# High halves of the weights by a converting DMA instead of a GpSimd pass, in a hybrid decoder trunk on one Trainium2 core

## The chip, the core and the metric

The kernel runs on one core of a Trainium2 chip. The metric is the device time of one execution in microseconds (us), the median of several runs. The engines are named as in the profile: PE is TensorE (PEld its weight loads), DVE is VectorE, ACT is ScalarE, POOL is GpSimd, SP is SyncE, and SPq and ACTq are the instructions with which SP and ACT issue DMAs. They run side by side and wait for each other on semaphores.

## The reference

Two layers of a decoder trunk over 512 tokens of width 2048, in float32. Each layer has one wide input projection, four parallel token mixers (linear attention, windowed attention, differential attention, gated delta rule), a gate on each, and one output projection added to the input:

```python
def hybrid_layer(x, norm_g, w_in, w_out, ...):
    h = rms_norm(x, norm_g)
    p = jnp.einsum('btd,dp->btp', h, w_in)               # 2048 x 7192 weights
    ...
    ya = gla_mixer(...) * jax.nn.silu(az)
    yb = swa_mixer(...) * jax.nn.silu(bz)
    yc = diff_mixer(...) * jax.nn.silu(cz)
    yd = gdn_mixer(...) * jax.nn.silu(dz)
    y = jnp.concatenate([ya, yb, yc, yd], axis=-1)
    return x + jnp.einsum('btm,md->btd', y, w_out)       # 2048 x 2048 weights

def reference(x, ...):
    for l in range(2):
        x = hybrid_layer(x, norm_g[l], w_in[l], w_out[l], ...)
    return x
```

The output is the (1, 512, 2048) array x. The time lies in the two projections and in the chains of small operations inside the mixers.

## The kernel before

**Precision by halves.** A projection in float32 is made of three matmuls on a reduced type that the program calls float32r. A weight w is split into a high half, w rounded to float32r, and a low half, w minus the high half. The activations are split in the same way (actT_hi, actT_lo). The product is hi*hi + hi*lo + lo*hi, so each tile of weights costs three matmuls for each block of 128 rows.

**The weight stream.** All weights of a layer lie in DRAM as a stream of k-tiles of 128x512 float32, two to a pair, 144 pairs a layer, 288 in all. SP loads pair i into the ring w_raw (RAW slots of a pair each) with one DMA of 512 KB (L313) and signals raw_in. POOL then makes both halves of each k-tile: L376 adds zero to w_raw and writes w_hi, which rounds it; L380 subtracts w_hi from w_raw and writes w_lo, and signals w_ready. The rings w_hi and w_lo have RING = 4 k-tiles each. POOL may write a k-tile's slot when PE has finished the k-tile four before it; PE signals this with kt_done, whose value starts at 4. After each pair POOL gives the slot of w_raw back through raw_used, on which SP waits (L311).

**The order on PE.** The function project runs one chunk of the projection: 16 k-tiles for the input (12 or 4 for the output), and for each k-tile 12 matmuls of 128x512 (four blocks of rows, three terms) on L421 into the accumulators acc[0] to acc[3]. Projections 0 to 3 of a layer run bare: the chunks dq, dk, dv of the gated delta rule, and dz. From projection 4 on, a generator (mixer) puts the matmuls of a mixer between those of the projection at fixed places: four projections with gdn, four with gla, two with swa, four output projections with dif, then four short ones of 4 k-tiles.

**What stands beside it.** A project may begin when acc[0] to acc[3] have been read out (acc_free). For dq, dk and dv DVE reads them out itself (turned_out, L1232) and then runs the convolution and its activation (conv): for each of four blocks of 128x512, a scaling (L1252), three shifted multiply-adds (L1256), an exponential on ACT (L916), an addition of one (L1260), a reciprocal (L1263) and a product (L1265). DVE's order is fixed by the text of the program: conv("dk") stands before turned_out("dv"). In gdn the first step of a block on PE (L451) waits for a product that DVE makes (AG, L1303); in swa PE (L660) waits for a copy by DVE (L1461) that stands behind a gate (L1197, L1199, L1201) and the normalisation of the next block (L1424, L1425, L1429).

**The start.** SP issues, in this order, two small constants, then x in four pieces of 1 MB (x_in, L309) with pairs 0 to 3 of the weights between them (L313). PE transposes x (turn_x, L729) before the first k-tiles, and again ahead of later ones.

Of the kernel before, what the change touches and what calls it, by code (L numbers as in the profile page):

```python
# [7 lines left out]
F32 = mybir.dt.float32  # L8
# [31 lines left out]
RAW, RING = 4, 4  # L40
# [73 lines left out]
def hybrid_trunk(nc, x, wstream, wsmall, pcol, prow, wlr, cf, masks, out):  # L114
    ctx = ExitStack()
    with ctx:
# [11 lines left out]
        w_hi = sb("w_hi", [P, RING, GW], F32R)  # L128
# [105 lines left out]
        raw_used, hi_done, w_ready = sem("raw_used"), sem("hi_done"), sem("w_ready")  # L234
# [68 lines left out]
        def _(sp):  # L303
# [7 lines left out]
            def weights(i):  # L311
                sp.wait_ge(raw_used, i + 1)
                sp.dma_start(w_raw[:, i % RAW].rearrange("p a n -> p (a n)"),  # L313
                             wstream[i:i + 1].rearrange("a p n -> p (a n)")).then_inc(raw_in[i % RAW], 16)
# [8 lines left out]
            weights(3)  # L323
# [10 lines left out]
        def _(pool):  # L334

            pool.sem_inc(raw_used, RAW)
# [25 lines left out]

            for l in range(DEPTH):
                for i in range(PAIRS):
                    s = i % RAW
# [5 lines left out]
                    pool.wait_ge(raw_in[s], (l * (PAIRS // RAW) + i // RAW) * 16 + 16)  # L371
                    for k in range(2):
                        n, r = 2 * i + k, (2 * i + k) % RING

                        pool.wait_ge(kt_done, l * LAYER_KTS + (n + 1))
                        pool.tensor_tensor(w_hi[:, r], w_raw[:, s, k], zeros[:, :].broadcast_to([P, GW]), ALU.add) \  # L376
                            .then_inc(hi_done, 1)

                        pool.wait_ge(hi_done, l * LAYER_KTS + (n + 1))
                        pool.tensor_tensor(w_lo[:, r], w_raw[:, s, k], w_hi[:, r].bitcast(F32),  # L380
                                           ALU.subtract).then_inc(w_ready, 1)

                    pool.wait_ge(w_ready, l * LAYER_KTS + (2 * i + 2))
                    pool.sem_inc(raw_used, 1)
# [3 lines left out]
        def _(pe):  # L388
# [7 lines left out]
            def project(l, q, kt0, kts, act_kt, turned=False, ahead=None, mixer=None, stages=1, skip=0,  # L396
# [5 lines left out]
                for k in range(kts):  # L402
                    if ahead:
                        ahead(k)
                    r = (kt0 + k) % RING

                    pe.wait_ge(w_ready, l * LAYER_KTS + (kt0 + k + 1))
                    for b in range(4):
# [5 lines left out]
                        if turned:  # L414
                            terms = [(w_hi[:, r, c], actT_hi[:, a]), (w_hi[:, r, c], actT_lo[:, a]),
                                     (w_lo[:, r, c], actT_hi[:, a])]
                        else:
                            terms = [(actT_hi[:, a, c], w_hi[:, r]), (actT_hi[:, a, c], w_lo[:, r]),
                                     (actT_lo[:, a, c], w_hi[:, r])]
# [1192 lines left out]
```

## Time and profile before

| | |
|---|---|
| median of 3 runs | 2127.36 us (2125.7 to 2127.44) |
| the profiled execution, its own time | 2127.9 us |
| its span in the profile | 2126.1 us |
| PE busy | 2038.3 us, 96% of the span |
| POOL busy | 1396.3 us, 66% |
| DVE busy | 1026.4 us, 48% |
| ACT busy | 537.6 us, 25% |
| DMA | 175.92 MB, 83 GB/s on average |
| granted PE clock, mean | 0.989 of full speed |

The span is what the profiler saw from the first to the last instruction; 1.8 us of the execution's time lie around it. Matmuls overlap each other, so the duration of one on the profile is longer than the step from one to the next. Idle time is counted before the instruction that ended it, with the instruction that released it. The granted clock is the share of full speed that TensorE's throttle allowed: 1.00 is 2.4 GHz and 0.50 is 1.2 GHz.

### The profile page before, as it was taken

What the parts mean: (1) busy time and instruction counts of PE and PEld (TensorE: products, weight loads), DVE (VectorE), ACT (ScalarE), POOL (GpSimd) and SP (SyncE); (2) the same over time, 40 slices, a digit from 0 to 9 for tenths busy, and PEclk for the clock granted to TensorE, in tenths of its full rate; (3) what the DMA queues carried; (4) which work ended last, traced back from release to release, by engine and by line L of the source; (5) the groups of instructions that cost most, each with busy time, mean ns of one, the idle gap of its engine ahead of it and who ended that gap; (6) DMA issues with size and microseconds to landing.
All of it is one profiled execution on the core that took longest, in us unless ns stands there. A gap on an engine that the chain in (4) does not pass through costs nothing.

```text
span 2126.1 us, 25561 instructions
## 1 busy us (share of the span) xinstructions
PE 2038.3 (96%) x10300; PEld 1660.6 (78%) x10300; DVE 1026.4 (48%) x1407; ACT 537.6 (25%) x1014; POOL 1396.3 (66%) x1164
## 2 busy tenths in 40 slices
PE   7998999999999989999999999999999999999999
PEld 6877878878888878767888778778778787776777
DVE  1699453453222455565427984435432225545563
ACT  4010221222222443332320112221222225423220
POOL 6797654555777756557787975545557777555676
PEclk9999999999999999999999999999999999999999
DMA  5232211211222211422442322111122222132223
GB/s 216 74 96 80 70 60 50 60 60 60 80 81 88 80 60 63 146 69 80 129 132 72 99 79 63 57 60 59 51 62 87 80 80 84 55 127 81 74 85 119
DMA packets 50709, 175.92 MB, mean 83 GB/s; under 512 B 5566, under 2 KB 6304, under 8 KB 49568
## 3 DMA queue, kind: packets, MB, share of 16 engines
q1 hardware_dynamic: 44288, 155.75, 23.3%
q10 hardware_dynamic: 6304, 18.55, 2.3%
q8 instruction: 81, 1.33, 0.3%
q14 instruction: 36, 0.29, 0.0%
HBM read 165.89 MB, written 8.39 MB: 82 GB/s over the span
## 4 chain that ended last, share of the span: by engine, by line
PE 72%; DVE 20%; ACT 5%; issue 2%; DMA 1%; SPq 0%; ACTq 0%
PE acc L421 55%; DVE slots L1256 3%; DVE slots L1199 3%; DVE general L1263 3%; PE mix L488 2%; PE mix L499 1%; PE mix L682 1%; PE mix L660 1%; PE mix L528 1%; PE mix L491 1%; DVE slots L1252 1%; ACT slots L849 1%; DVE general L1319 1%; DVE slots L1429 1%; PE mix L774 1%
## 5 line engine op out<-in xcount | busy, mean ns | idle before, releaser
L376 POOL TENSOR_TENSOR w_hi<-w_raw,zeros 128x512 fp32r<-128x512 f32 x576 | 626.2, 1087 | 671.5 <-PE acc L421 648.2
L421 PE MATMUL acc<-w_hi,actT_hi 128*128 128x512 f32 x1920 | 789.0, 411 | 14.0 <-DVE slots L1232 12.1
L380 POOL TENSOR_TENSOR w_lo<-w_raw,w_hi 128x512 fp32r<-128x512 f32 x576 | 767.6, 1333 | 45.1
L421 PE MATMUL acc<-w_hi,actT_lo 128*128 128x512 f32 x1920 | 755.3, 393 | 0.0
L421 PE MATMUL acc<-w_lo,actT_hi 128*128 128x512 f32 x1920 | 753.5, 392 | 0.0
L421 PEld LDWEIGHTS acc<-w_hi,actT_hi 128*128 128x128 f32 x1920 | 364.9, 190 | 106.6 <-issue 38.7
L421 PEld LDWEIGHTS acc<-w_hi,actT_lo 128*128 128x128 f32 x1920 | 363.2, 189 | 80.3
L421 PEld LDWEIGHTS acc<-w_lo,actT_hi 128*128 128x128 f32 x1920 | 365.3, 190 | 65.5
L421 PE MATMUL acc<-actT_hi,w_hi 128*128 128x512 f32 x384 | 153.2, 399 | 2.9 <-DVE slots L1232 2.9
L421 PE MATMUL acc<-actT_hi,w_lo 128*128 128x512 f32 x384 | 150.4, 392 | 0.0
L421 PE MATMUL acc<-actT_lo,w_hi 128*128 128x512 f32 x384 | 150.4, 392 | 0.0
L849 ACT ACTIVATE slots<-acc,xr 128x512 f32<-128x512 f32 x88 | 60.2, 689 | 267.8 <-PE acc L421 267.7
L1199 DVE RECIPROCAL slots<-slots 128x512 f32<-128x512 f32 x32 | 107.3, 3353 | 1.1
L1256 DVE SCALAR_TENSOR_TENSOR slots<-slots,pcol_all 128x511 f32<-128x511 f32 (+2 forms) x72 | 99.1, 1376 | 2.6
L421 PEld LDWEIGHTS acc<-actT_hi,w_hi 128*128 128x128 f32 x384 | 72.7, 189 | 18.8 <-issue 2.2
L421 PEld LDWEIGHTS acc<-actT_hi,w_lo 128*128 128x128 f32 x384 | 72.6, 189 | 15.5
L421 PEld LDWEIGHTS acc<-actT_lo,w_hi 128*128 128x128 f32 x384 | 72.7, 189 | 15.0 <-issue 0.5
L1263 DVE RECIPROCAL general<-general 128x512 f32<-128x512 f32 x24 | 80.5, 3353 | 0.8
L916 ACT ACTIVATE general<-slots 128x512 f32<-128x512 f32 x24 | 15.2, 632 | 252.8 <-DVE slots L1256 252.8
L974 ACT ACTIVATE slots<-mix 128x512 f32<-128x512 f32 x40 | 24.0, 599 | 216.1 <-PE mix L488 216.1
L1480 DVE TENSOR_TENSOR slots<-acc,slots 128x512 f32<-128x512 f32 x64 | 42.7, 688 | 67.4 <-PE acc L421 67.4
L1376 DVE SCALAR_TENSOR_TENSOR slots<-mix,slots 128x256 f32<-128x256 f32 x8 | 3.4, 424 | 139.7 <-ACT slots L999 139.7
(250 smaller groups left out, 2095.5 us busy)
## 6 DMA issues: line engine op xcount, KB each, us to landing
w_raw<-in_wstream SPq DMA_DIRECT2D x288, 512.0 KB, 3.5
out_x<-slots ACTq DMA_DIRECT2D x7, 1024.0 KB, 4.4
slots<-in_x SPq DMA_DIRECT2D x4, 1024.0 KB, 14.5
slots<-in_x ACTq DMA_DIRECT2D x1, 4096.0 KB, 14.2
slots<-out_x ACTq DMA_DIRECT2D x1, 4096.0 KB, 15.0
out_x<-slots ACTq DMA_DIRECT2D x4, 256.0 KB, 2.3
cf_sb<-in_cf ACTq DMA_DIRECT2D x1, 964.0 KB, 11.4
slots<-in_masks ACTq DMA_DIRECT2D x1, 384.0 KB, 12.2
```

The lines of the kernel that those rows point to most:

```text
L376: pool.tensor_tensor(w_hi[:, r], w_raw[:, s, k], zeros[:, :].broadcast_to([P, GW]), ALU.add) \
L380: pool.tensor_tensor(w_lo[:, r], w_raw[:, s, k], w_hi[:, r].bitcast(F32), ALU.subtract).then_inc(w_ready, 1)
L421: last = nc.tensor.matmul(acc[b][:, :], lhsT, rhs, start=(k == 0 and i == 0), stop=(k == kts - 1 and i == 2))
L488: last = nc.tensor.matmul(mh[3][:, h], U["MT"][:, h], U["X"][:, h], start=True, stop=True)
L491: last = nc.tensor.transpose(mh[1][:, h], U["X"][:, h], ident)
L499: last = nc.tensor.matmul(mh[0][:, h], U["XT"][:, h], U["Y"][:, h], start=True, stop=True)
L849: nc.scalar.activation(slot(SLOT[c])[:, b], acc[b][:, :], ACT.Copy, scale=xr[:, l, b:b + 1]) \
L974: nc.scalar.activation(U["Y"], mh[3], ACT.Copy).then_inc(*s(f"y{lv}"))
L1199: dve.reciprocal(tmp, tmp).then_inc(St.sem, St.one(f"{t}.g2"))
L1256: dve.scalar_tensor_tensor(dst[:, d:], src[:, 0:SEQ - d], tap[i], dst[:, d:], ALU.mult, ALU.add).then_inc(*ci(f"t{i}"))
L1263: dve.reciprocal(general[:, b % 2], general[:, b % 2]).then_inc(*ci("rec"))
L1480: dve.tensor_tensor(xs, acc[b][:, :], xs, ALU.add).then_inc(acc_free, 1)
```

## The change

The pass that makes the high half (L376) is gone from POOL. Instead POOL issues, for each pair, a second DMA from the same place in DRAM, from float32 into the float32r tile w_hi, so that the DMA converts. Only POOL's queue issues such a DMA here. w_hi becomes a ring of HI = 3 pairs with a semaphore for each slot (hi_in); w_raw shrinks from 4 pairs to 3, w_lo keeps its 4 k-tiles. The DMA for pair g + 1 is issued after the low half of the first k-tile of pair g; from g + 1 = 3 on it first waits until PE has finished the pair that held its slot. SP no longer waits for raw_used: it waits for w_ready, the low halves of the pair three before. PE only reads the high half from its new place.

```diff
-RAW, RING = 4, 4
+RAW, HI, RING = 3, 3, 4
...
-        w_hi = sb("w_hi", [P, RING, GW], F32R)
+        w_hi = sb("w_hi", [P, HI, 2, GW], F32R)
...
-        raw_used, hi_done, w_ready = sem("raw_used"), sem("hi_done"), sem("w_ready")
+        hi_in = [sem(f"hi_in{i}") for i in range(HI)]
+        w_ready = sem("w_ready")
...
             def weights(i):
-                sp.wait_ge(raw_used, i + 1)
+                if i >= RAW:
+                    sp.wait_ge(w_ready, 2 * (i - RAW) + 2)
                 sp.dma_start(w_raw[:, i % RAW].rearrange("p a n -> p (a n)"),
                              wstream[i:i + 1].rearrange("a p n -> p (a n)")).then_inc(raw_in[i % RAW], 16)
...
             x_in(3)
-            weights(3)
...
+            def high_halves(g):
+
+                if g >= HI:
+                    pool.wait_ge(kt_done, RING + 2 * (g - HI) + 2)
+                pool.dma_start(w_hi[:, g % HI].rearrange("p a n -> p (a n)"),
+                               wstream[g:g + 1].rearrange("a p n -> p (a n)")).then_inc(hi_in[g % HI], 16)
+
+            high_halves(0)
             for l in range(DEPTH):
                 for i in range(PAIRS):
-                    s = i % RAW
+                    g = l * PAIRS + i
...
-                    pool.wait_ge(raw_in[s], (l * (PAIRS // RAW) + i // RAW) * 16 + 16)
+                    pool.wait_ge(raw_in[g % RAW], g // RAW * 16 + 16)
+                    pool.wait_ge(hi_in[g % HI], g // HI * 16 + 16)
                     for k in range(2):
-                        n, r = 2 * i + k, (2 * i + k) % RING
-
-                        pool.wait_ge(kt_done, l * LAYER_KTS + (n + 1))
-                        pool.tensor_tensor(w_hi[:, r], w_raw[:, s, k], zeros[:, :].broadcast_to([P, GW]), ALU.add) \
-                            .then_inc(hi_done, 1)
-
-                        pool.wait_ge(hi_done, l * LAYER_KTS + (n + 1))
-                        pool.tensor_tensor(w_lo[:, r], w_raw[:, s, k], w_hi[:, r].bitcast(F32),
+                        n = 2 * g + k
+
+                        pool.wait_ge(kt_done, n + 1)
+                        pool.tensor_tensor(w_lo[:, n % RING], w_raw[:, g % RAW, k], w_hi[:, g % HI, k].bitcast(F32),
                                            ALU.subtract).then_inc(w_ready, 1)
-
-                    pool.wait_ge(w_ready, l * LAYER_KTS + (2 * i + 2))
-                    pool.sem_inc(raw_used, 1)
+                        if k == 0 and g + 1 < DEPTH * PAIRS:
+                            high_halves(g + 1)
...
-                    r = (kt0 + k) % RING
+                    n = l * LAYER_KTS + kt0 + k
+                    hi, lo = w_hi[:, n // 2 % HI, n % 2], w_lo[:, n % RING]
```

**POOL in the middle of a projection.** Before, one pair is four passes, and the next pair begins with the fifth row:

```order
L376 TENSOR_TENSOR w_hi<-w_raw,zeros 128x512 [waits w_ready,kt_done,raw_in3]
L380 TENSOR_TENSOR w_lo<-w_raw,w_hi 128x512 [waits hi_done]
L376 TENSOR_TENSOR w_hi<-w_raw,zeros 128x512 [waits kt_done]
L380 TENSOR_TENSOR w_lo<-w_raw,w_hi 128x512 [waits hi_done]
L376 TENSOR_TENSOR w_hi<-w_raw,zeros 128x512 [waits w_ready,kt_done,raw_in0]
```

After the change, one pair is two passes and the issue of a DMA (L367), which fetches the high halves of the next pair; the fourth row is the next pair's first:

```order
L385 TENSOR_TENSOR w_lo<-w_raw,w_hi 128x512 [waits kt_done,hi_in0,raw_in0]
L367 DMA w_hi<-in_wstream 128x1024 [waits kt_done]
L385 TENSOR_TENSOR w_lo<-w_raw,w_hi 128x512 [waits kt_done]
L385 TENSOR_TENSOR w_lo<-w_raw,w_hi 128x512 [waits kt_done,hi_in1,raw_in1]
L367 DMA w_hi<-in_wstream 128x1024 [waits kt_done]
```

Two passes that read SBUF have gone from each pair, and the first pass of a pair now also waits for a DMA (hi_in) that POOL issued one pass before.

**POOL at the start of the program.** Before, POOL waits for the first pair of weights with nothing issued:

```order
L338 MEMSET zeros 128x1
L339 MEMSET ws_hl 128x80
L376 ISA
L376 TENSOR_TENSOR w_hi<-w_raw,zeros 128x512 [waits kt_done,raw_in0,zeros_done]
L380 TENSOR_TENSOR w_lo<-w_raw,w_hi 128x512 [waits hi_done]
```

After it, the DMA of pair 0 goes out first:

```order
L338 MEMSET zeros 128x1
L339 MEMSET ws_hl 128x80
L367 DMA w_hi<-in_wstream 128x1024 [waits zeros_done]
L385 ISA
L385 TENSOR_TENSOR w_lo<-w_raw,w_hi 128x512 [waits kt_done,hi_in0,raw_in0]
L367 DMA w_hi<-in_wstream 128x1024
L385 TENSOR_TENSOR w_lo<-w_raw,w_hi 128x512 [waits kt_done]
```

The half megabyte of pair 0 (high) now moves beside the first pieces of x, and that of pair 1 follows after POOL's first pass, without a wait. On SP the fourth load of weights, which stood right behind the last piece of x, now waits for w_ready.

## Rows read from the trace of the kernel before

**Rows 1.** The page: busy time, share of the span, instructions.

```profile
PE 2038.3 (96%) x10300; PEld 1660.6 (78%) x10300; DVE 1026.4 (48%) x1407; ACT 537.6 (25%) x1014; POOL 1396.3 (66%) x1164
```

**Rows 2.** The chain that ended last: start us, us, what.

```profile
174.27 8.45 PE acc L421 x24
183.52 43.66 PE acc L421 x192
...
555.84 23.34 PE acc L421 x102
...
607.14 23.34 PE acc L421 x102
...
756.31 6.09 PE acc L421 x18
```

**Rows 3.** Waits of PE: who waited for whom: us in total, times, longest.

```profile
PE mix L660 <- DVE slots L1461: 20.0, 6, 3.9
PE acc L421 <- DVE slots L1232: 15.0, 4, 6.1
PE mix L729 <- DMA slots<-in_x: 14.1, 2, 10.4
PE mix L451 <- DVE slots L1303: 10.9, 6, 1.8
PE mix L682 <- DVE slots L1495: 8.9, 2, 4.5
```

**Rows 4.** Timeline of PE: start, us, instruction, in brackets idle time before and releaser.

```profile
124.39 0.47 PE L421 MATMUL acc<-actT_hi,w_hi 128*128 128x512 f32 x1 [1.57 <-DVE slots L1232]
...
174.27 0.76 PE L421 MATMUL acc<-w_hi,actT_hi 128*128 128x512 f32 x1 [6.08 <-DVE slots L1232]
...
754.26 2.05 PE L660 MATMUL mix<-slots 128*128 128x128 f32 x8 [3.86 <-DVE slots L1461]
```

**Rows 5.** Timeline of DVE in conv("dk") and at the start of conv("dv").

```profile
160.66 1.52 DVE L1252 TENSOR_SCALAR slots<-slots,pcol_all 128x512 f32<-128x512 f32 x1
162.21 4.65 DVE L1256 SCALAR_TENSOR_TENSOR slots<-slots,pcol_all 128x511 f32<-128x511 f32 x3
...
175.84 0.47 DVE L1252 TENSOR_SCALAR slots<-slots,pcol_all 128x512 f32<-128x512 f32 x1
176.34 2.32 DVE L1256 SCALAR_TENSOR_TENSOR slots<-slots,pcol_all 128x511 f32<-128x511 f32 x3
```

**Rows 6.** Timeline in gdn and swa; L1201's durations, ns min/median/max.

```profile
300.24 1.04 POOL L376 TENSOR_TENSOR w_hi<-w_raw,zeros 128x512 fp32r<-128x512 f32 x1 [0.24 <-PE acc L421]
300.25 1.57 DVE L1303 TENSOR_TENSOR slots<-cf_sb,glog 128x512 f32<-128x512 f32 x1
...
L1201 DVE TENSOR_TENSOR slots<-slots x32: 691/1320/1800, 279.0 to 2063.6; 128x512 f32<-128x512 f32 x32
...
747.44 1.00 DVE L1455 TENSOR_TENSOR stat<-stat 128x4 f32<-128x4 f32 x1
```

**Rows 7.** Groups of POOL: count, busy us, mean ns, idle time before and releasers.

```profile
L380 POOL TENSOR_TENSOR w_lo<-w_raw,w_hi 128x512 fp32r<-128x512 f32 x576 | 767.6, 1333 | 45.1
L376 POOL TENSOR_TENSOR w_hi<-w_raw,zeros 128x512 fp32r<-128x512 f32 x576 | 626.2, 1087 | 671.5 <-PE acc L421 648.2 <-DMA w_raw<-in_wstream 13.2 <-POOL w_lo L380 9.6
```

**Rows 8.** The page's DMA issues and SP's queue; L313's issue times, ns min/median/max.

```profile
w_raw<-in_wstream SPq DMA_DIRECT2D x288, 512.0 KB, 3.5
...
q1 hardware_dynamic: 44288, 155.75, 23.3%
...
L313 SPq DMA_DIRECT2D w_raw<-in_wstream x288: 327/328/6001, 2.1 to 2092.6; - x144
```

**Rows 9.** The start: a window (busy us, clock, DMA share, GB/s), and PE's timeline.

```profile
10.00:15.00 5.00, 3.65 (x16) 3.27 (x16) 1.27 (x2) 3.39 (x5) 0.91 (x1) 1.00 1.01 408
...
10.43 3.65 PE L729 MATMUL mix<-cf_sb,slots 128*128 128x128 f32 x16 [10.43 <-DMA slots<-in_x]
...
17.75 1.09 PE L729 MATMUL mix<-cf_sb,slots 128*128 128x128 f32 x4 [3.68 <-DMA slots<-in_x]
```

More of the change, by code:

```diff
@@ L334, in _ @@
         def _(pool):
-            pool.sem_inc(raw_used, RAW)
             pool.sem_inc(ws_ready, 1)
@@ L414, in project @@
                         if turned:
-                            terms = [(w_hi[:, r, c], actT_hi[:, a]), (w_hi[:, r, c], actT_lo[:, a]),
-                                     (w_lo[:, r, c], actT_hi[:, a])]
-                        else:
-                            terms = [(actT_hi[:, a, c], w_hi[:, r]), (actT_hi[:, a, c], w_lo[:, r]),
-                                     (actT_lo[:, a, c], w_hi[:, r])]
+                            terms = [(hi[:, c], actT_hi[:, a]), (hi[:, c], actT_lo[:, a]), (lo[:, c], actT_hi[:, a])]
+                        else:
+                            terms = [(actT_hi[:, a, c], hi), (actT_hi[:, a, c], lo), (actT_lo[:, a, c], hi)]
                         for i, (lhsT, rhs) in enumerate(terms):
```

## The prediction, made before the changed kernel was timed

> **What bounds the kernel now.** I read the page's busy shares first [rows 1]: PE is busy for 96% of the span, so POOL at 66% is not what sets the time on average. Then the chain that ended last, for PE's pace: 192 matmuls of the projection take 43.66 us [rows 2], 0.2274 us each. A k-tile is 12 of them, 2.73 us, and a pair of k-tiles 5.46 us. POOL's two passes for a k-tile take 1.09 + 1.33 = 2.42 us [rows 7], so POOL keeps up, and most of its idle time (648 us) ends with PE. Third, the waits of PE [rows 3]: nearly all of what is not matmul. 14.1 us are for x at the start; the rest is for DVE: 20.0 us in swa (L1461), 15.0 us for an accumulator that DVE reads out late (L1232), 10.9 us in gdn (L1303), 8.9 us in dif. So the time can fall only if DVE's chains get shorter, and it can rise if weights come late, which costs up to the whole difference in pace.
>
> Why DVE is late stands in [rows 5]: three multiply-adds of conv take 4.65 us beside a working POOL and 2.32 us once POOL has stopped; a scaling takes 1.52 and 0.47 us. In [rows 6] a DVE product starts 0.01 us after a POOL pass of 1.04 us and takes 1.57 us, where such a product takes 0.69 us at the least, and a 128x4 operation takes 1.00 us. DVE's operations wait for the POOL pass under way. The Trainium skill, SBUF — State Buffer, section Who interferes with whom, says that a DVE instruction with two SBUF inputs or in a two-port mode and a GpSimd instruction share a port pair as a lock; these rows agree.
>
> **What the change removes, and what that gives.** POOL loses 576 passes, 626 of its 1394 us of passes [rows 7]: 45% of the time in which DVE can be blocked.
>
> (a) conv. The excess in a block is 4.65 - 2.32 + 1.52 - 0.47 = 3.4 us [rows 5], 13.5 us in the four blocks of dk. PE waits 6.08 us for dk's end and 1.57 us for dq's [rows 4], nearly the same in the second layer (the sum of all four is 15.0 us [rows 3]). 45% of 13.5 us is 6.1 us: the wait would just go. As collisions are not spread evenly, I count 5 of the 6.08 us, and the 1.57 us: 6.5 us a layer, 13 us. What is late next there is nothing: PE then runs on at its pace. After the wait PE runs at a lowered clock: 24 matmuls take 8.45 us [rows 2] where 24 x 0.2274 = 5.5 us, 3.0 us more. A wait of about 1 us leaves the clock alone, as after the wait of 1.57 us, so I count 2 x 2.9 = 5.7 us. Together 18.7 us. Ends: 3 and 21 us.
>
> (b) gdn. L1303 starts with the POOL pass that the same k-tile releases [rows 6]. That pass is the second of a pair (n odd), and there the new order puts the DMA's issue ahead of the subtraction. So the product runs free: 1.57 - 0.69 = 0.88 us less, six times: 5.3 us. If the issue blocks DVE too: 0.
>
> (c) swa. Six waits, 20.0 us. On the way to L1461 stand L1201, L1455, L1424 and L1429, all of them held up: L1201's median is 1.32 us against 0.69 us, L1455 took 1.00 us [rows 6]. I take 1.3 us off each wait, 8 us, and 2 us for the clock after them (18 matmuls took 6.09 us instead of 4.1 after the wait of 3.86 us [rows 2, 4]). Ends: 0 and 18 us. The waits in dif I leave: no POOL pass stands beside the operations before them.
>
> (d) The start. From 10 us on the DMA engines are full (share 1.01, 408 GB/s) [rows 9], and PE's first two steps wait for x until 10.43 and 17.75 us. 0.52 MB more ahead of the second piece are 1.3 us, and a part of pair 1's high half follows: +2 us. Ends: 0 and 4. The load of pair 3 that SP no longer sends at once isn't needed until k-tile 6.
>
> Gains less the start: 18.7 + 5.3 + 10 - 2 = 32 us.
>
> **What the change adds: a loop on POOL.** POOL waits for the high half of pair g, makes the first low half (1.33 us), then issues the DMA for g + 1, and does not get past the next wait until it has landed. Only one such DMA is in flight. Let A be the time from its issue to its landing. Then POOL's pair takes A + 1.33 us, however little POOL works, and must fit in 5.46 us: A may be 4.13 us. Behind the waiting POOL stand the low halves, and behind these PE and SP's loads.
>
> What A is, no row shows; the nearest ones bound it. SP's load of the same 512 KB, unconverted, takes 3.5 us to land, 0.33 us of it the issue [rows 8]: the lower end, 3.5 us. POOL writes its descriptors in software; I price this as one pass of POOL, 1.09 us [rows 7], in place of 0.33: A = 4.26 us, and I take this. For the upper end, converting halves the rate: 23.3% of 2126 us for 155.75 MB [rows 8] is 1.67 us of all engines for 512 KB, so 1.67 us more, A = 5.93 us. The Trainium skill, DMA: Bandwidth & Descriptors, section Latency and other measured facts, gives about 1 us to the first byte from GpSimd and about 0.6 us from SP; by this A would be 3.9 us and the loop would cost nothing; no run here shows it.
>
> The loss: PE can use up a lead of 10.9 - 5.5 = 5.4 us (four k-tiles of w_lo less the loop) before it starves. Bare stretches at 5.46 us a pair are projections 0 to 3 (32 pairs a layer) and the 8 short last pairs, which in layer 0 run into the next layer: 32 and 40 pairs. gla's pairs come at (607.14 - 555.84)/8 = 6.41 us [rows 2], gdn's slower. With A = 4.26 us the loop is 0.13 us too long: 72 x 0.13 = 9.4 us, less than the two leads (10.8 us). Loss 0. The loads of w_raw keep three pairs: they are issued five k-tiles (13.6 us) before use and need 3.5 us. POOL's masks and small weights move only behind the DMA issues ahead of them and are not late.
>
> Against the profiled execution, 2127.9 us (span 2126.1 us and 1.8 us around it, 0.5 us above the median): 2127.9 - 32 = **2096 us**.
>
> **Rivals.**
> 1. *Forecast*: A up to 4.5 us, DVE's waits shrink. 2078 to 2112 us, likeliest 2096. For it: [rows 5, 6]. Chance 0.42.
> 2. *The loop is somewhat too long.* A DVE operation that takes the port as POOL begins to write descriptors holds the DMA back: in conv there are two short scalings a block (0.47 us each [rows 5]), about one a pair, and w_lo's pass is held up as well. A = 4.5 to 5.2 us; at 4.8 the loop is 0.67 us too long, 72 x 0.67 - 10.8 = 37 us, so 2096 + 37 = 2133 us; its ends are 2112 and 2162 us. Break-even with before is A = 4.72 us. The Trainium skill has this mechanism on the page SBUF — State Buffer, section SBUF: two separate sides, as descriptor starvation, and tells authors to issue from SP or ACT. Chance 0.22.
> 3. *Slower: the converting DMA is slow.* Place: the wait for hi_in in the bare projections, where PE waits for L385 each pair. It decides from A = 4.72 us. At half rate A = 5.93 us, the loop is 7.26 us, 1.80 us too long: 72 x 1.80 - 10.8 = 119 us, and in gla 0.85 x 32 - 5.4 = 22 us a layer. 2096 + 119 + 43 = 2258 us. For it: this is the first DMA in the kernel that converts, and the loop has no depth to hide a slow one. Against it: the engines are idle for three quarters of the span. Chance 0.18.
> 4. *Much slower*: quarter rate or below, 5 us more than in the forecast. The loop is 10.6 us and sets the pace of all 288 pairs: 3050 us. Chance 0.08.
> 5. *It does not do what it could*: writing descriptors holds the port as long as the pass did, or DVE meets the remaining low-half passes instead. DVE's waits stay, the start costs 2 us: 2130 us. Against it: two passes are replaced by one issue in each pair. Chance 0.10.
>
> **How the numbers follow.** A measurement of this kernel can tell 0.2% (4 us) from no change. Faster: all of 1 (0.42) and 0.06 of 2: 0.48. Within 0.2%: 0.05 of 2 and 0.07 of 5: 0.12. Slower: 0.11 of 2, 0.18, 0.08 and 0.03 of 5: 0.40. The range runs from 2078 us, where (a) to (c) come near their upper ends, to 2260 us, case 3 at half rate. It leaves out case 4, what of case 3 is slower than half rate (0.06) and 0.03 below. As both signs hold much of the chance: the forecast's own range is 2078 to 2112 us.
>
> **What the profile after would show.** For the loop: the time from issue to landing of w_hi in the DMA issues, under 4.5 us; no wait of PE for POOL's L385 in the bare projections; 192 matmuls still in 43.7 us. For (a): L1256 well under its mean of before, no wait of PE at the first matmul of project 2 or 3 over 1 us, the clock at full there. For (b): PE's wait for L1303 near 0.9 us instead of 1.8 us. For (c): waits for L1461 of about 2 us. For (d): x's second piece at 19 to 20 us instead of 17.75. The forecast is wrong if w_hi takes over 4.7 us to land (then PE waits on POOL, and w_ready sets the pace), or if DVE's operations stay as long as before.

## The result, and the profile after

The changed kernel takes 2077.56 us (median of 4 runs, 2076.23 to 2081.78), the kernel before 2126.53 us on the same chip (4 runs, 2125.17 to 2127.44): a ratio of 0.9774 with a 95% interval from 0.9757 to 0.9791, so 49 us or 2.3% faster. It is the side that was forecast, with more gain than the 32 us of the sum; the time lies 0.4 us below the low end of the range (2078 us). The profiled execution took 2081.78 us, the slowest of the four; its span is 2080.0 us, 46.1 us less than before's.

The page of the kernel after answers [rows 1], [rows 7] and [rows 8]: busy times, the two queues that carry weights (packets, MB, share of 16 engines), POOL's low-half group, and the DMA issues (KB, us to landing).

```profile
PE 2022.2 (97%) x10300; PEld 1651.9 (79%) x10300; DVE 955.8 (46%) x1407; ACT 536.4 (26%) x1014; POOL 924.9 (44%) x876
...
q0 software_dynamic: 41472, 151.01, 25.0%
q1 hardware_dynamic: 44288, 155.75, 24.4%
...
L385 POOL TENSOR_TENSOR w_lo<-w_raw,w_hi 128x512 fp32r<-128x512 f32 x576 | 759.4, 1319 | 761.7 <-DMA w_hi<-in_wstream 439.1
...
w_hi<-in_wstream POOLq DMA_DIRECT2D x288, 512.0 KB, 3.8
w_raw<-in_wstream SPq DMA_DIRECT2D x288, 512.0 KB, 4.4
```

POOL works 471 us less. 439 us of its idle time now end with the landing of w_hi; as much as 647 us (271 before a low half, 375 before an issue) still end with PE. DVE does the same 1407 instructions in 70.6 us less. The converting DMA lands 3.8 us after its issue.

The waits of PE answer [rows 3] (old lines L729, L660, L682, L421, L451 are L732, L663, L685, L424, L454 now):

```profile
PE mix L732 <- DMA slots<-in_x: 15.5, 2, 14.6
PE mix L663 <- DVE slots L1464: 11.8, 6, 3.7
PE mix L685 <- DVE slots L1498: 8.3, 2, 4.2
PE acc L424 <- DVE slots L1235: 7.0, 2, 3.6
PE mix L454 <- DVE slots L1306: 5.6, 6, 1.0
```

No wait on POOL is among them. The waits of L663 fell from 20.0 to 11.8 us, of L424 for the read-out from 15.0 to 7.0 us and of L454 from 10.9 to 5.6 us. One wait of before that no step of the prediction named is gone altogether. In the profile of before it read:

```profile
PE mix L528 <- DVE general L1352: 6.6, 8, 0.8
```

The chain after answers [rows 2]:

```profile
169.28 7.13 PE acc L424 x24
177.21 43.66 PE acc L424 x192
```

And the timeline of PE after answers [rows 4, 9]: its waits for the second piece of x and at the first k-tile of project 3, which is dz.

```profile
19.11 0.63 PE L732 MATMUL mix<-cf_sb,slots 128*128 128x128 f32 x4 [0.83 <-DMA slots<-in_x]
...
169.28 0.77 PE L424 MATMUL acc<-w_hi,actT_hi 128*128 128x512 f32 x1 [3.56 <-DVE slots L1235]
```

PE's pace is the same (192 matmuls in 43.66 us). To see where the 46.1 us lie, I set the start of each of the 10300 matmuls beside that of the same matmul before, and read the difference where a stage ends:

| stage | predicted | measured, both layers |
|---|---|---|
| (a) conv: waits of project 2 and 3, clock behind them | 18.7 us | 5.7 + 5.0 = 10.7 us |
| (b) gdn | 5.3 us | 8.9 + 8.8 = 17.7 us |
| gla | 0 | 0 |
| (c) swa: waits, clock behind them | 10 us | 8.3 + 9.0 = 17.3 us |
| (d) start | -2 us | +0.6 us |
| dif | 0 | -0.7 + 0.5 = -0.2 us |

The sum is 46.1 us. Three stages give 10.7 to 17.7 us each, where I had put most of the gain into the first.

### The profile page after: what moved, and what is told of

It is laid out like the page before. It is cut to its first block, busy times and chain, and to the rows that moved or that the text cites. A ratio compares the mean times of both kernels' runs of the same rounds, so it can differ in the third digit from the quotient of the medians.

```text
span 2080.0 us, 24984 instructions
## 1 busy us (share of the span) xinstructions
PE 2022.2 (97%) x10300; PEld 1651.9 (79%) x10300; DVE 955.8 (46%) x1407; ACT 536.4 (26%) x1014; POOL 924.9 (44%) x876
## 3 DMA queue, kind: packets, MB, share of 16 engines
q8 instruction: 81, 1.33, 0.2%
## 4 chain that ended last, share of the span: by engine, by line
PE 84%; DVE 8%; ACT 6%; issue 1%; DMA 1%; SPq 0%; ACTq 0%
PE acc L424 65%; PE mix L491 2%; PE mix L502 1%; DVE general L1266 1%; DVE slots L1259 1%; PE mix L685 1%; PE mix L494 1%; PE mix L531 1%; PE mix L524 1%; DMA slots<-in_x 1%; PE mix L663 1%; ACT slots L852 1%; ACT L1044 1%; ACT L1041 1%; PE mix L777 1%
## 5 line engine op out<-in xcount | busy, mean ns | idle before, releaser
L385 POOL TENSOR_TENSOR w_lo<-w_raw,w_hi 128x512 fp32r<-128x512 f32 x576 | 759.4, 1319 | 761.7 <-DMA w_hi<-in_wstream 439.1
L424 PE MATMUL acc<-w_hi,actT_hi 128*128 128x512 f32 x1920 | 786.0, 409 | 8.9 <-DVE slots L1235 7.0
L424 PE MATMUL acc<-w_hi,actT_lo 128*128 128x512 f32 x1920 | 753.6, 393 | 0.0
L424 PE MATMUL acc<-w_lo,actT_hi 128*128 128x512 f32 x1920 | 751.3, 391 | 0.0
L424 PEld LDWEIGHTS acc<-w_hi,actT_hi 128*128 128x128 f32 x1920 | 363.1, 189 | 101.0 <-issue 33.3
L424 PEld LDWEIGHTS acc<-w_hi,actT_lo 128*128 128x128 f32 x1920 | 361.9, 188 | 79.4
L424 PEld LDWEIGHTS acc<-w_lo,actT_hi 128*128 128x128 f32 x1920 | 363.8, 189 | 64.8
L367 POOL DMA_DIRECT2D w_hi<-in_wstream x288 | 163.7, 568 | 382.8 <-PE acc L424 375.3
L424 PE MATMUL acc<-actT_hi,w_hi 128*128 128x512 f32 x384 | 152.0, 396 | 0.0
L424 PE MATMUL acc<-actT_hi,w_lo 128*128 128x512 f32 x384 | 149.7, 390 | 0.0
L424 PE MATMUL acc<-actT_lo,w_hi 128*128 128x512 f32 x384 | 149.5, 389 | 0.0
L424 PEld LDWEIGHTS acc<-actT_hi,w_hi 128*128 128x128 f32 x384 | 72.1, 188 | 15.3 <-issue 0.9
L424 PEld LDWEIGHTS acc<-actT_hi,w_lo 128*128 128x128 f32 x384 | 72.1, 188 | 15.3
L424 PEld LDWEIGHTS acc<-actT_lo,w_hi 128*128 128x128 f32 x384 | 72.2, 188 | 14.9 <-issue 0.5
L1259 DVE SCALAR_TENSOR_TENSOR slots<-slots,pcol_all 128x511 f32<-128x511 f32 (+2 forms) x72 | 73.0, 1014 | 2.5
```

Source lines behind the costliest of these rows:

```text
L367: pool.dma_start(w_hi[:, g % HI].rearrange("p a n -> p (a n)"), wstream[g:g + 1].rearrange("a p n -> p (a n)")).then_inc(hi_in[g % HI], 16)
L385: pool.tensor_tensor(w_lo[:, n % RING], w_raw[:, g % RAW, k], w_hi[:, g % HI, k].bitcast(F32), ALU.subtract).then_inc(w_ready, 1)
L424: last = nc.tensor.matmul(acc[b][:, :], lhsT, rhs, start=(k == 0 and i == 0), stop=(k == kts - 1 and i == 2))
L1259: dve.scalar_tensor_tensor(dst[:, d:], src[:, 0:SEQ - d], tap[i], dst[:, d:], ALU.mult, ALU.add).then_inc(*ci(f"t{i}"))
```

## The experiments

Each ratio is against the kernel before, timed beside it on the same chip (medians of 2126.7 to 2127.2 us); the changed kernel's own 2077.56 us stand beside 2126.53 us. Where a text below compares two runs by stage, the numbers are the differences of the matmuls' start times in the two profiled executions, both layers together, read as in the table above.

**1. The relief without the DMA.** The kernel before, POOL's first pass cut from 512 to 8 columns (the rest of w_hi stays zero and w_lo carries the weight).

```diff
...
-  pool.tensor_tensor(w_hi[:, r], w_raw[:, s, k], zeros[:, :].broadcast_to([P, GW]), ALU.add) \
+  pool.tensor_tensor(w_hi[:, r, 0:8], w_raw[:, s, k, 0:8], zeros[:, :].broadcast_to([P, 8]), ALU.add) \
```

> The kernel before, with POOL's pass for the high half cut from 512 to 8 columns (w_hi is zeroed once at the start and its other columns stay zero, so most of the high halves are left out of the products). No second DMA, rings as before. Theory 1 (the gain of the change is the read port: DVE no longer waits for that pass): 2070 to 2085 us, about 45 us under the kernel before; L1256 near 1.0 us in the mean instead of 1.38, PE's waits for DVE like those after the change. Theory 2 (the gain comes from elsewhere, from the new rings or from weights that are there earlier): 2120 us or more.

Measured: 2068.28 us, ratio 0.9725 [0.9711, 0.974], 58.5 us faster than before and 9.3 us faster than the changed kernel. From its page, and then from its waits of PE:

```profile
PE 2021.1 (98%) x10300; PEld 1652.3 (80%) x10300; DVE 911.9 (44%) x1407; ACT 536.1 (26%) x1014; POOL 912.4 (44%) x1165
```

```profile
PE mix L730 <- DMA slots<-in_x: 14.1, 2, 10.2
```

Without any new DMA the whole gain is there: it comes from the passes that left POOL. DVE is busy for another 44 us less than in the changed kernel, and the wait for L1235 (7.0 us there) is gone. x is there at 10.2 us, as before. What the changed kernel gives back is about 9 us. It is not lost at the start: between the two profiled executions (12.9 us) 10.6 us lie in conv and 3.6 us in swa, while the changed kernel is 0.8 us ahead in the first projection. Many high halves are zero here, so the matmuls work on other data; the mean granted clock, 0.994, is that of the changed kernel's profiled execution.

**2. A reading pass put back.** The changed kernel with a pass of 128x512 that reads w_raw ahead of each low half, and nothing else.

```diff
                         pool.wait_ge(kt_done, n + 1)
+                        pool.tensor_tensor(w_lo[:, n % RING], w_raw[:, g % RAW, k], zeros[:, :].broadcast_to([P, GW]),
+                                           ALU.add).then_inc(dummy_done, 1)
+                        pool.wait_ge(dummy_done, n + 1)
                         pool.tensor_tensor(w_lo[:, n % RING], ...
```

> The changed kernel, with a pass put back ahead of each low half: it adds zero to w_raw and writes the slot of w_lo, which the subtraction then overwrites. The result is unchanged. Theory 1 (port): the gain goes, 2118 to 2140 us; DVE's L1259 back at 1.35 us or more; a little above the kernel before is possible because the loop on POOL (wait for w_hi 3.8 us, two passes 2.4 us) is then 6.2 us for a pair where bare projections need 5.46. Theory 2: up to 2085 us.

Measured: 2191.16 us, ratio 1.0301 [1.0283, 1.032], 114 us over the changed kernel and far above what I expected. The two longest waits of PE:

```profile
PE mix L667 <- DVE slots L1468: 27.3, 6, 6.1
PE acc L428 <- POOL w_lo L389: 24.8, 34, 2.9
```

Two things are mixed here: DVE's waits are back (27.3 us in swa), and PE now waits for the low halves. The next two runs take them apart.

**3. The same time on POOL without reading.** Two memsets of 0.54 us in place of the reading pass.

```diff
+                        pool.memset(w_lo[:, n % RING].bitcast(F32), 0.0).then_inc(dummy_done, 1)
+                        pool.wait_ge(dummy_done, 2 * n + 1)
+                        pool.memset(w_lo[:, n % RING].bitcast(F32), 0.0).then_inc(dummy_done, 1)
+                        pool.wait_ge(dummy_done, 2 * n + 2)
```

> The changed kernel, with two memsets of the w_lo slot ahead of each low half, so that POOL is busy about as long as with the old pass but reads nothing from SBUF. The result is unchanged. If DVE waits only for passes that read SBUF (theory 1a): L1259 stays near 1.0 us and the time is that of the changed kernel plus what the longer loop costs (two memsets of 0.4 to 0.5 us ahead of the first low half make it 3.8 + 1.0 + 1.3 = 6.1 us, 0.65 us over the bare pace: up to 35 us). If any work of POOL holds DVE up (theory 1b): L1259 at 1.3 us or more, 2125 us or more, as with the pass that reads.

Measured: 2138.54 us, ratio 1.0061 [1.0043, 1.0078]. Its page, its waits of PE, and POOL's timeline in a bare projection, in this order:

```profile
PE 2051.4 (96%) x10300; PEld 1648.4 (77%) x10300; DVE 928.4 (43%) x1407; ACT 536.3 (25%) x1014; POOL 1525.3 (71%) x2028
```

```profile
PE acc L429 <- POOL w_lo L390: 24.7, 47, 2.4
PE mix L668 <- DVE slots L1469: 12.0, 6, 2.7
```

```profile
67.48 0.57 POOL L367 DMA_DIRECT2D w_hi<-in_wstream  x1
68.05 0.55 POOL L385 MEMSET w_lo<- 128x512 f32 x1
...
73.64 0.57 POOL L367 DMA_DIRECT2D w_hi<-in_wstream  x1
```

POOL is as busy as in experiment 2, yet DVE's 928.4 us and the 12.0 us in swa are those of the changed kernel or better. So what holds DVE up is above all that the pass reads, and the 53 us between experiments 2 and 3 are its price; by stage they lie in swa (25 us), gdn (20 us) and conv (7 us). The memsets are not quite without effect: of DVE's operations with two inputs none that meets only memsets is over 0.02 us longer than its least, but some with one input (the scalings and additions, TENSOR_SCALAR) are, by up to 0.43 us.

The 61 us over the changed kernel (54.7 us between the profiled executions) are mostly the loop: from issue to issue it takes 73.64 - 67.48 = 6.16 us, more than the 5.46 us of PE's pair. The prediction's formula gives 72 x (6.16 - 5.46) - 10.8 = 40 us for it, and 40 us are what the stretches without a mixer lost: 10.7 in projection 0, 22.2 in projections 1 to 3, 7.5 in the short last ones. Another 10 us lie in gdn and are not the loop: the memsets move the low-half pass onto the product that PE waits for (L1311 here, median 1.64 us; PE waits 11.5 us for it, 5.6 us in the changed kernel).

**4. The loop made longer.** The changed kernel with the DMA for g + 1 issued after the second low half of pair g.

```diff
-                        if k == 0 and g + 1 < DEPTH * PAIRS:
+                        if k == 1 and g + 1 < DEPTH * PAIRS:
                             high_halves(g + 1)
```

> The changed kernel, with the DMA for pair g + 1 issued after the second low half of pair g instead of after the first. Theory L (POOL's loop of one DMA in flight sets the pace of the bare projections once it is longer than 5.46 us): the loop is 3.8 + 2 x 1.32 = 6.4 us, 0.98 us too long, 72 pairs x 0.98 less two leads of 5.4 us = 60 us, so 2130 to 2145 us, with PE waiting for the low half (L385) in projections 0 to 3. Rival (weights have more lead than I count): 2075 to 2090 us.

Measured: 2336.24 us, ratio 1.0985 [1.0969, 1.1001], 259 us over the changed kernel. The waits of PE, the DMA issue on the page, and POOL's timeline:

```profile
PE acc L424 <- POOL w_lo L385: 187.8, 137, 5.0
```

```profile
w_hi<-in_wstream POOLq DMA_DIRECT2D x288, 512.0 KB, 4.9
```

```profile
137.89 0.57 POOL L367 DMA_DIRECT2D w_hi<-in_wstream  x1
142.97 2.69 POOL L385 TENSOR_TENSOR w_lo<-w_raw,w_hi 128x512 fp32r<-128x512 f32 x2 [4.51 <-issue]
145.61 0.57 POOL L367 DMA_DIRECT2D w_hi<-in_wstream  x1
```

From issue to issue it is 7.7 us here. The median over all pairs is 7.58 us: 4.9 us of landing and two passes. Two errors of my expectation are in it. The landing is not 3.8 but 4.9 us: at this place POOL's DMA goes out in the same moment as SP's load of w_raw, which the same low half releases. And the loss is taken wherever PE's pair is shorter than 7.58 us, not in the bare stretches and gla alone: from the starts of the DMA issues, the first layer lost 55 us in pairs 0 to 31, 33 in gla, 10 in swa and 32 in the output projections with the short last pairs, 0 in gdn. In both layers the bare pairs lost 133 us (the formula's bare term gives 142) and gla 69 us (64); swa and dif, some 50 us, were missing from it.

**5. Two DMAs in flight, issued at the same late place.** w_hi has 4 pairs and w_raw 2 (together as many as in the changed kernel); the DMA for g + 2 goes out where that for g + 1 did in experiment 4.

```diff
-RAW, HI, RING = 3, 3, 4
+RAW, HI, RING = 2, 4, 4
...
-                        if k == 1 and g + 1 < DEPTH * PAIRS:
-                            high_halves(g + 1)
+                        if k == 0 and g == 0:
+                            high_halves(1)
+                        if k == 1 and g + 2 < DEPTH * PAIRS:
+                            high_halves(g + 2)
```

> The same two DMAs in flight, but issued after the second low half of a pair, as in the kernel of 2336 us that had only one in flight there. POOL's work is the same in both. Loop theory (what cost 258 us was only that POOL waits for a landing in each pair): all of it comes back, 2070 to 2090 us, and no long list of PE waits on the low halves. Rival (the two loads of a pair, released by the same low half at the same moment, slow each other down, landing 4.9 us and more): the collision stays, and if it was the cause the time stays above 2150 us; the landing time in the DMA issues tells whether it stays.

Measured: 2080.27 us, ratio 0.9788 [0.9773, 0.9802]. All of the 256 us came back. Its DMA issue, its waits, the chain, and the timeline of POOL and DVE in gdn:

```profile
w_hi<-in_wstream POOLq DMA_DIRECT2D x288, 512.0 KB, 4.9
```

```profile
PE mix L455 <- DVE slots L1307: 12.2, 6, 2.0
PE mix L664 <- DVE slots L1465: 8.3, 6, 2.3
...
PE acc L425 <- DVE slots L1236: 2.1, 2, 1.1
```

```profile
165.91 5.69 PE acc L425 x24
```

```profile
287.53 1.26 POOL L384 TENSOR_TENSOR w_lo<-w_raw,w_hi 128x512 fp32r<-128x512 f32 x1 [1.34 <-PE acc L425]
287.55 1.79 DVE L1307 TENSOR_TENSOR slots<-cf_sb,glog 128x512 f32<-128x512 f32 x1
288.74 0.57 POOL L366 DMA_DIRECT2D w_hi<-in_wstream  x1
```

The landing is still 4.9 us, so the collision of the two loads costs nothing once POOL does not stand still for it. In experiment 4 POOL waited for one landing in each pair, and the collision had a share in the loss only by making that loop 1.1 us longer. The run also bears out step (b). With the issue behind the second low half, the product of gdn (here L1307) meets the pass again: 1.79 us, and PE waits 12.2 us for it, as before the change (10.9 us). In the changed kernel the issue stands ahead of that pass, and the same product runs almost at its least. Its timeline:

```profile
292.37 0.71 DVE L1306 TENSOR_TENSOR slots<-cf_sb,glog 128x512 f32<-128x512 f32 x1
292.57 0.57 POOL L367 DMA_DIRECT2D w_hi<-in_wstream  x1
293.16 1.28 POOL L385 TENSOR_TENSOR w_lo<-w_raw,w_hi 128x512 fp32r<-128x512 f32 x1
```

In conv it goes the other way: the wait for the read-out is 2.1 us instead of 7.0, and 24 matmuls behind it take 5.69 us, full pace. Against the first kernel of experiment 6, which has the same rings and issues after the first low half, this one loses 14.8 us in gdn and gains 10.6 us in conv, 3.1 in swa, 1.5 in dif and 1.4 in the first projection. What the place of the issue takes in one stage it gives in another, and the sums are alike.

**6. Two in flight at the place of the change, and its control.** With the DMA for g + 2 issued after the first low half (`if k == 0`), and the changed kernel with only `RAW = 2`.

> The changed kernel with two converting DMAs in flight: w_hi has 4 pairs, w_raw 2 (the memory has no room for more), and the DMA for pair g + 2 is issued where that for g + 1 was. Landing then has about 10 us instead of 4.1 us. Loop theory: in the changed kernel the loop of 3.8 + 1.3 = 5.1 us fits into PE's 5.46 us, so one in flight costs nothing and this gives 2070 to 2082 us, with no new wait of PE on the low halves. Rival: one in flight still costs something hidden in late low halves after each stall; then up to 10 us less, 2066 to 2070 us. Second rival: two pairs of w_raw are too few; then PE waits on low halves and the time is over 2085 us.

> The changed kernel with w_raw of 2 pairs instead of 3 and nothing else, the control for the two kernels with two DMAs in flight: what the smaller ring costs by itself. The load of w_raw is then released one pair (5.46 us) before its first use instead of two, and lands in 4.4 us. If it fits: 2074 to 2084 us, as the changed kernel, perhaps 1 to 3 us less at the start, because the third load no longer stands ahead of x's last piece. If not: PE waits on the low halves, POOL on w_raw, and the time is 2100 us or more.

Measured: 2080.81 us, ratio 0.9781 [0.9765, 0.9798], and 2077.92 us, ratio 0.9778 [0.9758, 0.9798]. Both are close to the changed kernel's time, the first 3 us above it. In the changed kernel the loop fits and one DMA in flight costs nothing that can be measured, though POOL waits 439 us for it; and two pairs of w_raw are enough.

**7. The reading pass once more, with two in flight.** Experiment 2 with the rings and the issue of experiment 6.

> The kernel of 2191 us (the changed kernel with a reading pass of 1.07 us put back ahead of each low half) with two converting DMAs in flight instead of one. The relief of the port is gone as there; what remains of the loop is gone too, and POOL's own work, 2 x (1.07 + 1.34) + 0.57 = 5.4 us a pair, is just under PE's 5.46 us, so POOL hardly gains a lead again after a stall. If the reading passes cost as much as the passes of before did and waiting for the landing cost the rest: about 2127 us plus the start and a little for the missing lead, 2122 to 2150 us. Rival (POOL's work, not the wait for a landing, was what 2191 us showed): 2175 us or more, with waits of PE on the low halves as there (24.8 us in 34 waits).

Measured: 2148.28 us, ratio 1.0098 [1.0081, 1.0115], 43 us under experiment 2 and at the top of what I expected. No wait of PE for a low half is left among the longest; they are for DVE. The longest:

```profile
PE mix L668 <- DVE slots L1469: 27.6, 6, 5.0
```

So 43 of experiment 2's 114 us hung on the single DMA in flight (by stage 32 us in the stretches without a mixer and 12 us in gdn), and 71 us are the lost relief. That is 21 us more than the kernel before has, with its same passes: DVE is busy 1063.3 us here and 1026.4 us there. By stage it lies in swa (10.8 us), conv (5.0) and dif (4.5). What makes DVE meet more of POOL's work here is not settled; that POOL's instructions stand at other places beside DVE's is likely, as in experiment 5, but no run tests it.

**8. The DMA alone, converting and not.** The kernel before with RAW = 3, both passes kept, and one DMA a pair by POOL into a tile that nobody reads, waited for as in the change; once into float32r, once into float32; and RAW = 3 alone. The cut leaves out the new tile, its semaphore and the first issue.

```diff
...
+            def extra(g):
+                pool.dma_start(w_extra[:, :], wstream[g:g + 1].rearrange("a p n -> p (a n)")).then_inc(extra_in, 16)
...
+                    pool.wait_ge(extra_in, 16 * (l * PAIRS + i) + 16)
...
+                        if k == 0 and l * PAIRS + i + 1 < DEPTH * PAIRS:
+                            extra(l * PAIRS + i + 1)
```

> The kernel before with w_raw at three pairs and, added, the change's converting DMA: POOL issues it after the first low half of each pair, into a tile that nobody reads, and waits for it before the next pair. Both passes stay on POOL. It measures the DMA without the relief. Its price by the change's own trace: POOL's loop is 3.8 us to landing and two passes of 2.4 us, 6.2 us, 0.75 us over the bare pace: 72 x 0.75 - 10.8 = 43 us at the most, 2127 to 2170 us. If issuing descriptors also blocked DVE, L1256 would rise over its 1.38 us of before; if not, it stays. Rival: the DMA is hidden altogether, 2125 to 2130 us.

> As e6_dma_alone, but the tile is float32, so that the DMA copies and does not convert. If converting costs nothing: the same time to landing (3.8 us), the same issue (0.57 us) and the same share of the DMA engines (25%), and the time of e6_dma_alone within 0.2%. If converting slows the DMA: landing under 3.5 us and a smaller share.

> The kernel before with w_raw at three pairs instead of four, nothing else. Expected: no change, 2125 to 2129 us: a load is issued five k-tiles (13.6 us) before use and lands in 3.5 us. If the ring's depth mattered, PE would wait for POOL and the time would rise.

Measured: 2176.45 us, ratio 1.0227 [1.021, 1.0244]; 2176.84 us, ratio 1.0238 [1.0223, 1.0253]; 2126.62 us, ratio 0.9997 [0.9987, 1.0006]. The queue of POOL and the landing, converting first, then plain:

```profile
q0 software_dynamic: 41472, 151.01, 23.9%
...
w_extra<-in_wstream POOLq DMA_DIRECT2D x288, 512.0 KB, 3.8
```

```profile
q0 software_dynamic: 41472, 151.01, 22.0%
...
w_extra<-in_wstream POOLq DMA_DIRECT2D x288, 512.0 KB, 3.8
```

The conversion costs nothing in landing or time. The engines' shares differ by 1.9 points, less than they do between runs with the same converting DMA (17.6% in experiment 4, 19.7% in 5, 25.0% in the changed kernel), so no price for converting can be read from them. Rival 3's reason, half the rate, doesn't hold. The 50 us that such a DMA costs a kernel that keeps both passes agree with experiments 2 and 3: 3.8 us of landing and 2.4 us of passes make a loop of 6.2 us; 36 us of the loss lie in the stretches without a mixer and 12 us in gdn.

**9. dv's read-out moved ahead.** In the changed kernel, turned_out("dv") stands before the last block of conv("dk"), to end the wait for L1235.

```diff
-                conv("dk", [1, 2, 3])
+                conv("dk", [1, 2])
...
                 turned_out("dv")
+                conv("dk", [3])
                 conv("dv", T)
```

> The changed kernel, with DVE reading out the accumulators of dv before the last block of conv for dk instead of after it. PE's two waits for L1235 (3.56 and 3.47 us) and the lowered clock after each (1.7 us) should go: 2077.6 - 10 = 2067 us, 2064 to 2072. What could be late instead: DVE stands idle for some 4 us until PE has finished dv, so conv for dv ends 4 us later; the first block of gdn needs it at about 221 us and has it at 213 us now. If that slack is less than it looks: 2072 to 2080 us, with a wait of PE at L454 of the first block.

Measured: 2084.37 us, ratio 0.9799 [0.9785, 0.9814], not faster than the changed kernel; a miss. The wait for L1235 went, and another took its place:

```profile
PE acc L424 <- ACT slots L852: 8.3, 2, 5.8
```

ACT takes out dz behind an activation of the convolution, which now comes later. A wait of PE is worth only the distance to the next one that ends late.

## Why the prediction was right, and where its sum was off

**The bound and the mechanism** were right. DVE's chains behind POOL's reading passes are what PE waits for: experiment 1 gains 58.5 us from shorter passes alone, experiment 3 shows that POOL work of the same length that doesn't read leaves DVE's busy time and the waits in swa where the change put them, and experiments 2 and 7 lose the gain when it reads. The Trainium skill, SBUF — State Buffer, section Who interferes with whom, has this lock between a GpSimd instruction that reads SBUF and a DVE instruction with two SBUF inputs. The traces agree (292.37: 0.71 us free; 287.55: 1.79 us behind a pass).

The total came out within 14 us of the sum in part by luck: conv gave 8 us less than counted, gdn 12.4, swa 7.3 and the start 2.6 us more, and these partly cancel.

**(a) conv was over-sized**: 10.7 us instead of 18.7. PE waits 3.56 us instead of 6.08 before project 3, so 2.5 us went where I counted 5; the clock behind it came back by 8.45 - 7.13 = 1.3 us a layer and not 2.9. The step that failed is that 45% less POOL work takes 45% of DVE's excess. In conv("dk") of the first layer the excess of the scalings, multiply-adds, additions and products over their least durations was 13.2 us before (13.5 were counted) and is 10.5 us after, 20% less. One operation got slower. The durations after (ns, min/median/max) of the multiply-adds and of the product:

```profile
L1259 DVE SCALAR_TENSOR_TENSOR slots<-slots,pcol_all x72: 749/751/1876, 78.6 to 1234.0; 128x511 f32<-128x511 f32 x24, 128x510 f32<-128x510 f32 x24, 128x509 f32<-128x509 f32 x24
...
L1268 DVE TENSOR_TENSOR slots<-slots,general x24: 691/2166/2276, 85.8 to 1240.7; 128x512 f32<-128x512 f32 x24
```

The multiply-adds mostly run free now, but the product that ends a block has a median of 2.17 us, where it had 0.69 before. The timeline after, in conv("dk"), shows one:

```profile
155.28 0.57 POOL L367 DMA_DIRECT2D w_hi<-in_wstream  x1
155.71 2.02 DVE L1268 TENSOR_TENSOR slots<-slots,general 128x512 f32<-128x512 f32 x1
155.88 1.30 POOL L385 TENSOR_TENSOR w_lo<-w_raw,w_hi 128x512 fp32r<-128x512 f32 x1
```

It starts while POOL issues the DMA, and is then held through the whole low-half pass, which begins 0.17 us later. This is a pattern. Of DVE's operations between SBUF tiles (0.4 us and longer, reciprocals left out), 31 start in the changed kernel during an issue that a pass follows, and 23 of them are held, by up to 1.6 us; 49 start beside an idle POOL just ahead of a pass, and 2 are held. In experiments 4 and 5, where no pass stands behind the issue, 55 start during an issue and none is held (0.08 us at the most). So the issue alone does not hold DVE; an issue with a reading pass right behind it mostly does, and the change put one into every pair. Experiment 5, with the issue elsewhere, has a median of 0.69 us for the product and 2.1 us of such waits of PE. Which operation is hit is a matter of timing: the first kernel of experiment 6 also has 0.69 us for the product, but 26 of 34 operations are held in this way, multiply-adds among them, and PE waits 8.2 us.

**(b) gdn was under-sized**: 17.7 us instead of 5.3. The term itself was exact: L454 waits 5.6 us instead of 10.9, 5.3 us less, and experiment 5 shows that it hangs on the place of the issue, as argued. Not in the sum were the waits for L1352 (6.6 us listed, 7.1 us from start to start, all gone) and for L971 and L1323 (1.4 and 3.2 us from start to start). Before, the gate's product L1201 ahead of L1352 took 1.32 us beside a POOL pass (the median of [rows 6]); after, as L1204, it takes 0.69 us. I read this line for swa and did not ask who waits behind it in gdn.

**(c) swa was under-sized**: 17.3 us instead of 10. The waits fell by 20.0 - 11.8 = 8.2 us, as counted (8). The clock was mis-sized: 9.1 us are left for it where 2 us were predicted. The window of swa in the first layer and one lowered stretch in it, before and then after (busy us of PE, PEld, DVE, ACT and POOL, then granted clock, DMA share, GB/s):

```profile
735.00:870.00 135.00, 124.51 (x616) 104.58 (x614) 72.21 (x104) 57.34 (x116) 79.38 (x67) 0.95 0.28 97
753.60:760.40 6.80, 6.14 (x19) 5.20 (x20) 1.64 (x6) 0.00 (x0) 0.00 (x0) 0.50 0.25 77
```

```profile
717.00:850.00 133.00, 125.70 (x640) 104.07 (x639) 69.56 (x110) 60.54 (x121) 54.28 (x52) 0.99 0.51 167
762.80:766.20 3.40, 3.19 (x15) 3.22 (x16) 0.06 (x1) 0.00 (x0) 0.00 (x0) 0.50 0.26 104
```

The clock rose from 0.95 to 0.99, and so it did in the second layer's 140 us: about 275 x 0.04 = 11 us at full speed, an estimate, and near the 9.1. Before, the clock was at 0.50 (1.2 GHz) three times in the first layer's window, for 6.8, 3.4 and 3.4 us; after, once, for 3.4 us. I had priced one lowered stretch behind one wait; shorter waits spared two more and half of the first.

**(d) The start** cost nothing, by luck: x's first piece came 4.2 us later (14.63 instead of 10.43), but the second at 19.11 instead of 17.75, and PE waits 0.83 us for it instead of 3.68 us. The first k-tile then starts 1.0 us later (19.50 instead of 18.49), as the step has it, but goes faster. Its second matmul, before and after:

```profile
19.06 0.63 PE L421 MATMUL acc<-actT_lo,w_hi 128*128 128x512 f32 x1
```

```profile
19.82 0.40 PE L424 MATMUL acc<-actT_lo,w_hi 128*128 128x512 f32 x1
```

Before, the matmuls of this k-tile follow each other at 0.43 us until 22.9 us, and at 0.23 us from then on; after, they do so at 0.23 us from the first. The k-tile takes 2.8 us instead of 5.0 us, and that is more than the late start. (The profile has a granted clock of 1.00 for both stretches; only the steps show the difference.) Experiment 1, which has no such DMA, gets x at 10.2 us.

**The loop.** A was 3.8 us for the 4.26 us taken, in the range of 3.5 to 5.93. The pair takes 3.8 + 1.33 = 5.1 us and fits into 5.46; no PE wait on POOL appeared, and experiment 6 finds nothing hidden. The estimate of 3.9 us that the prediction drew from the Trainium skill, DMA: Bandwidth & Descriptors, section Latency and other measured facts, was nearer than my bound by one POOL pass; the issue takes 0.57 us.

**The break-even.** That one DMA in flight is a limit showed at once when 1.1 us was added (experiments 2, 3 and 8, 43 to 61 us) or 2.4 us (experiment 4, 259 us). Break-even with before was given as A = 4.72 us. Experiment 3, whose loop of 6.16 us is that of A = 4.83 us, lies 12 us above before, so break-even is somewhat below 4.8 us, an estimate. That this is so near the number given is partly luck: the gain was 17 us larger than the sum, and a loop that is too long cost some 10 us in gdn besides the formula's 40.

**The rivals.** 2 (descriptors held up by DVE): the landing had a median of 3.8 us; nothing of it showed. 3 and 4 (slow conversion): ruled out by experiment 8. 5 (no relief): ruled out by the 70.6 us less of DVE, and the issue alone holds nothing (experiments 4 and 5); its second half, that DVE meets the remaining passes instead, is true of conv in part (L1268). The chance of 0.40 for slower hung mostly on one unknown, A; what a loop that is too long costs, experiments 3 and 4 show. The range's low end, 2078 us, was too near: waits outside the three steps could add gain, and I left no room for them.

## What to carry to other kernels

When POOL loses reading passes, list every DVE operation that was longer than its minimum beside them, and follow each to the one who waits for it, in every stage; the gain lay in waits of 0.2 to 0.9 us, taken 8 times, as much as in the one of 6 us. A load whose landing the issuing engine awaits before it goes on is a loop: write down issue to landing plus the work between, compare it with the consumer's pace in each stage, and remember that a loop 0.7 us too long cost 43 to 61 us here, and that depth two made the landing time not matter. When an issue moves, which DVE operations meet the next pass changes too, so compare stages and not only totals, and look for a reading pass that stands right behind an issue on the same engine.

## What the runs showed that I had not expected

- A GpSimd pass that only writes (memset, 0.54 us for 128x512) leaves DVE's operations with two inputs alone and holds some TENSOR_SCALAR operations by up to 0.43 us: DVE is busy 928.4 us beside 1152 of them and 1065.7 us beside 576 reading passes of 1.07 us.
- A converting DMA costs no more to land than a plain one (3.8 us both for 512 KB).
- Two loads of 512 KB issued in the same moment by SP and POOL: w_raw lands in 3.6 us and w_hi in 4.9 us. In the changed kernel, where POOL's goes out first, they take 4.4 and 3.8 us; with one more pass of POOL in between (experiment 2) 3.5 and 3.8 us.
- A DVE product that begins during POOL's issue, 0.17 us ahead of the reading pass behind it, is held through that pass (2.02 us instead of 0.69); during an issue with no pass behind it, none of 55 was.
